# Forgetting attention: who parts queries and keys of head pairs 2 to 7 into a high and a low half

## The reference

```python
def fox_mixer(xn, w_q, w_o, k, v, c):
    q = (xn @ w_q).reshape(B, T, B_HEADS, HEAD_DIM)        # T = 512, 16 heads of 64
    for i in range(T // BLK):                              # 4 blocks of 128 queries
        q0, q1 = i * BLK, (i + 1) * BLK
        s = einsum('bqhd,bkhd->bhqk', q[:, q0:q1], k[:, :q1]) * scale
        s = s + (c_t[:, :, q0:q1, None] - c_t[:, :, None, :q1])
        s = where(causal, s, NEG)
        p = softmax(s, axis=-1)
        outs.append(einsum('bhqk,bkhd->bqhd', p, v[:, :q1]))
    return concatenate(outs, axis=1).reshape(B, T, B_WIDTH) @ w_o
```

## Time and profile before

| | |
|---|---|
| median of 3 runs | 3076.61 us (3074.89 to 3082.62) |
| profiled execution, span from its first to its last instruction | 3080.3 us |
| PE busy | 2933.2 us, 95% of the span |
| DVE busy | 1776.7 us, 58% |
| ACT busy | 1435.4 us, 47% |
| POOL (GpSimd) busy | 538.9 us, 17% |
| the 32 units of `fox` | about 2535 to 2655 us of the span |

### The profile page before, as it was taken

How to read it: one execution, slowest core, us unless ns; L and a number is a source line. 1 busy time by engine, 2 the same in 40 slices (tenths; PEclk the granted TensorE clock), 3 DMA queues, 4 the chain that set the end, 5 groups by cost and what they waited for, 6 DMA issues and landing times. The chain is left out here.

```text
span 3080.3 us, 38613 instructions
## 1 busy us (share of the span) xinstructions
PE 2933.2 (95%) x15514; PEld 2375.0 (77%) x15514; DVE 1776.7 (58%) x1996; ACT 1435.4 (47%) x1913; POOL 538.9 (17%) x626
## 2 busy tenths in 40 slices
PE   8999999898999999999999899999999998899998
PEld 4878888786887578777777478788888896688887
DVE  4448755546644788888888264555544326455543
ACT  3345525437223478888787133533333325443332
POOL 0016513224101633323222100000001002000000
PEclk9999999999999999999999999999999998899999
DMA  5220111021762599999999551233332310233331
GB/s 206 55 64 1 45 46 56 28 56 59 229 196 87 205 336 371 362 370 373 372 380 355 219 197 47 55 97 96 103 103 69 113 39 32 76 89 96 96 101 44
DMA packets 278385, 456.07 MB, mean 148 GB/s; under 512 B 24864, under 2 KB 206752, under 8 KB 258112
## 3 DMA queue, kind: packets, MB, share of 16 engines
q1 hardware_dynamic: 251712, 398.82, 37.5%
q0 software_dynamic: 26496, 54.79, 4.9%
HBM read 451.16 MB, written 39.08 MB: 159 GB/s over the span
## 5 line engine op out<-in xcount | busy, mean ns | idle before, releaser
L264 DVE TENSOR_TENSOR weight_part<-weights,weight_part 128x2048 fp32r<-128x2048 f32 (+1 forms) x62 | 140.6, 2267 | 157.0 <-ACT weight_part L253 157.0
L1193 ACT ACTIVATE up_conv<-banks,tap_columns 128x512 f32<-128x512 f32 x88 | 68.5, 778 | 292.4 <-PE banks L311 292.4
L253 ACT ACTIVATE weight_part<-weights 128x2048 fp32r<-128x2048 f32 (+1 forms) x62 | 116.0, 1871 | 172.7 <-PE banks L306 167.2
L781 POOL TENSOR_SCALAR branch_mean<-branch_mean 128x1 f32<-128x1 f32 x20 | 10.4, 521 | 1059.0 <-ACT up_conv L775 713.3
L1237 DVE SCALAR_TENSOR_TENSOR up_conv<-banks,tap_columns,up_conv 128x511 f32<-128x511 f32 x88 | 65.9, 749 | 218.0 <-ACT up_conv L1193 218.0
L306 PE MATMUL banks<-hT_r,weight_part 128*128 128x512 f32 x448 | 176.5, 394 | 0.3 <-PEq L3857 0.3
L311 PE MATMUL banks<-hT_r,weight_part 128*128 128x512 f32 x448 | 175.6, 392 | 0.0
L264 DVE TENSOR_TENSOR weight_part_o<-weights,weight_part_o 128x2048 fp32r<-128x2048 f32 (+2 forms) x46 | 100.0, 2175 | 117.8 <-ACT weight_part_o L253 117.8
L3310 POOL DMA_INDIRECT gathered<-h_tokens,block_rows x64 | 115.6, 1806 | 203.6 <-PE banks L3427 189.1
L306 PE MATMUL banks<-hT_r,weight_part_o 128*128 128x512 f32 x384 | 151.0, 393 | 0.0
L311 PE MATMUL banks<-hT_r,weight_part_o 128*128 128x512 f32 x384 | 150.2, 391 | 0.0
(11 more groups left out here) (728 smaller groups left out, 8888.6 us busy)
## 6 DMA issues: line engine op xcount, KB each, us to landing
weights<-in_w_e_gate SPq DMA_DIRECT2D x44, 1024.0 KB, 15.6
weights<-in_w_e_up SPq DMA_DIRECT2D x44, 1024.0 KB, 18.2
hT<-in_w_e_down SPq DMA_DIRECT2D x44, 1024.0 KB, 18.6
weights<-in_w_up SPq DMA_DIRECT2D x88, 512.0 KB, 5.2
gate_up<-in_w_e_gate SPq DMA_DIRECT2D x22, 1024.0 KB, 15.6
gate_up<-in_w_e_up SPq DMA_DIRECT2D x22, 1024.0 KB, 18.3
down<-in_w_e_down SPq DMA_DIRECT2D x22, 1024.0 KB, 18.3
weights<-in_w_down SPq DMA_DIRECT2D x20, 1024.0 KB, 5.0
```

What stands on the lines that cost most here:

```text
L253: c.nc.scalar.activation(self.pair(n)[0][:, 0:z], self.raw[n % RAW_SLOTS][:, 0:z], ACT.Copy).then_inc(self.high_ready, 1)
L264: c.nc.vector.tensor_tensor(low[:, 0:z], self.raw[n % RAW_SLOTS][:, 0:z], high[:, 0:z].bitcast(F32), ALU.subtract).then_inc(self.low_ready, 1)
L1193: nc.scalar.activation(a[:, f % 2, v], c.ps[:, 2 * (f % 4) + v], ACT.Identity, scale=conv[:, 2, ch:ch + 1], bias=bias[:, ch:ch + 1]).then_ ...
```

## The change

GpSimd keeps `prepare(0)` and `prepare(1)`. For pairs 2 to 7 its loop is gone. The high parts are made by ScalarE (`FoxRoom.high`): the keys' behind the exponentials of unit `4 (f - 1) + 1`, the queries' behind those of unit `4 (f - 1) + 2`. The low parts are made by VectorE (`FoxRoom.low`), at the end of its work of unit `4 (f - 1) + 2` for the keys and of unit `4 (f - 1) + 3` for the queries. TensorE waits for both low parts (`parted`) ahead of the first scores of pair `f`.

```diff
+    def high(self, c, act, f, x):
+
+        part, whole = ((self.kp, self.kT), (self.qp, self.qT))[x]
+        c.nc.scalar.activation(part[f % 2][:, 0], whole[:, f], ACT.Copy).then_inc(self.rounded, 1)
+
+    def low(self, c, dve, f, x):
+
+        part, whole = ((self.kp, self.kT), (self.qp, self.qT))[x]
+        dve.wait_ge(self.rounded, 2 * (f - 2) + x + 1)
+        c.nc.vector.tensor_tensor(part[f % 2][:, 1], whole[:, f], part[f % 2][:, 0].bitcast(F32), ALU.subtract).then_inc(self.parted, 1)
...
         def _(pool):
             room.prepare(c, pool, 1)
-            for f in range(2, KD):
-                pool.wait_ge(scored, NT * (f - 1))
-                room.prepare(c, pool, f)
...
-                    if i == 0:
+                    if i == 0 and f < 2:
                         pe.wait_ge(room.prepared, 4 * (f + 1))
+                    elif i == 0:
+                        pe.wait_ge(room.parted, 2 * (f - 1))
...
+                if n < U and n % NT in (1, 2) and 2 <= n // NT + 1 < KD:
+                    if n % NT == 1:
+                        act.wait_ge(scored, n - 1)
+                    room.high(c, act, n // NT + 1, n % NT - 1)
...
                     nc.vector.tensor_tensor(oT[1][:, f], c.ps[:, 6 + f % 2], oT[0][:, f].bitcast(F32), ALU.subtract).then_inc(left, 1)
+                if n < U and n % NT in (2, 3) and 2 <= n // NT + 1 < KD:
+                    room.low(c, dve, n // NT + 1, n % NT - 2)
```

More of the change, by code:

```diff
@@ L1382, in __init__ @@
         self.prepared = c.sem("fox_prepared")
+        self.rounded, self.parted = c.sem("fox_rounded"), c.sem("fox_parted")
     def more(self, c):
```

## The result

| | before | changed |
|---|---|---|
| median | 3078.84 us (4 runs, 3074.89 to 3082.62) | 3100.92 us (4 runs, 3098.75 to 3107.11) |
| ratio, 95% interval | | 1.0071 (1.0055 to 1.0086) |
| span of the profiled execution | 3080.3 us | 3105.4 us |
| start of the stage (pair 0's last 128x1024 maximum) | 2541.07 | 2551.83 |
| the stage, to pair 7's maximum | 98.75 us | 113.60 us |

The change makes the kernel 22 us slower. The direction and the stall are as predicted. The size was not: I had 14.0 us, and the median lies 2.9 us above the range; the term that failed is the slow clock's, and some 3 us lie outside the stage. Two profiles decompose their own difference exactly: 10.8 us in the start of the stage, 14.85 in the stage, -0.5 behind it.

What follows compares the result with a forecast made beforehand. GpSimd's subtractions delay VectorE's divisions, stalling PE and lowering its clock. Stage 11.17 + 6 x (11.17 + 3.91 stall + 1.85 clock) = 112.8 against 98.75 us; 3076.6 + 14.0 = 3090.6 us, range 3083 to 3098.

Steps and rivals of the forecast that it cites:

- What bound the kernel before: At six pair boundaries GpSimd's subtractions delay VectorE's divisions; PE stalls 1.58 us each; removing all would gain 20.6 us.
- What is hidden: ScalarE's roundings fit its idle gaps and the keys' subtraction fits VectorE's 1.44 us idle time; they cost nothing.
- The stall: Ahead of the first scores of pairs 2 to 7, PE waits 3.91 us for VectorE's queries' subtraction.
- that place: Queries' subtraction directly behind the division, ahead of the low output part: stall of 1.97 us.
- The clock: Behind each of six stalls PE's slow clock costs 1.85 us, the mean cost in the kernel before.
- My bound of 2.90: Upper bound in this stage for the slow clock's cost behind each stall, giving 20.3 us more in sum.
- The sum again: Stage from 98.75 to 112.8 us: one clean boundary and six with stall and slow clock, 14.0 us more.
- No difference: Rival: the stall comes but the slow clock costs under 1.05 us a boundary; 3079.5 to 3085.8 us, chance 0.18.
- Faster: Rival: the queries' low part is there before PE asks; 3056 us with all of it hidden, chance 0.03.
- No effect on the divisions: Rival: VectorE's long divisions have another cause than GpSimd and stay; 3098 us, chance 0.01.
- The rule set against it: Skill's advice of VectorE for elementwise work, GpSimd about twice as slow; by it alone a 20.6 us gain.

Runs made afterwards that it cites:

- pool_two_units_later: Kernel before, with GpSimd's wait for pairs 2 to 7 moved two units later; 3066.06 us, ratio 0.9949.
- pool_casts_only: Kernel before, keeping GpSimd's casts but leaving out its subtractions for pairs 2 to 7; 3063.22 us, ratio 0.9938.
- no_parting: Changed kernel without the parting of pairs 2 to 7 and PE's wait for it (leaves out work); 3065.69 us, ratio 0.9946.
- one_unit_earlier: Changed kernel with all roundings and subtractions of the parting one unit earlier; 3066.1 us, ratio 0.9947.
- the full-clock stages: For the changed kernel, the 100.23 us stage of it with 17 idle multiplications of the identity ahead of PE's wait for the parts; 3088.88 us, ratio 1.0024.
- changed_again: Changed kernel, unedited, timed and profiled again; 3103.61 us, ratio 1.0077, stage 121.83 us.
- double_subtraction_2: Changed kernel with the queries' subtraction done twice; 3118.98 us, ratio 1.0110.
- before_output_part: Changed kernel with the queries' subtraction ahead of the low output part and its wait for ScalarE; 3096.53 us, ratio 1.0040.
- samples 1 and 2: Kernel before, unedited, two further profiled executions; single-run times 3091.39 and 3083.76 us.
- the fourth profile of the changed kernel: Changed kernel, unedited, profiled once more; single-run time 3104.71 us, stage 113.65 us.

## What was right in the prediction, and the term that failed

**What bound the kernel before.** Right. GpSimd's subtractions held up the divisions; moving them (pool_two_units_later) or leaving them out (pool_casts_only) took 16 to 19 us off, against the 20.6 that I gave for the stage (its stage shrinks by 17 to 19 us from the mean of four profiles).

**What is hidden.** Right: no wait, no growth for the roundings and the keys' subtraction; no_parting and one_unit_earlier have the same stage.

**The stall.** Predicted 3.91 us each; the timeline has 3.84, and 3.71 at full clock net of idle time. Set against before's 1.45 (I had 1.58), the six make 6 x (3.71 - 1.45) = 13.6 us where the sum's stall terms came to 14.0. The layout by hand was good to 0.1 us, and it named the deciding chain: with the low output part and its wait for ScalarE out of the way the stall is 1.8 us, near the 1.97 that I gave for that place.

**The clock: the step that failed.** I took "the mean cost of now, 1.85 us", for the stalls before and after alike, so that the term fell out of the difference. With the full-clock stages as zero, it measures in the changed kernel (113.60 - 100.23) / 6 = 2.2 to (121.83 - 100.23) / 6 = 3.6 us, in the mean of four profiles (115.73 - 100.23) / 6 = 2.6; in the kernel before, whose full-clock stage would be 77.98 + 6 x 1.45 = 86.7, from 1.0 to 2.0, in the mean of four (96.95 - 86.7) / 6 = 1.7. So behind the new stall the clock costs some 0.9 us more at each boundary, 5.2 us in all. My bound of 2.90 came from the stalls of then; the mean of 2.6 lies inside it, changed_again's 3.6 does not.

That the greater length of the stall is the reason is not shown. Reckoned in the same way, with its own stall added to the 77.98 us, double_subtraction_2 pays most, (133.73 - 77.98 - 6 x 4.44) / 6 = 4.9 us behind 4.6 us; but before_output_part pays (107.59 - 77.98 - 6 x 1.69) / 6 = 3.2 us behind only 1.8, more than three of the four profiles of the changed kernel. Its stall stands where the changed kernel's does, ahead of the scores, while that of the kernel before stands ahead of the transposes. The place, or the moment at which the stall falls, may count as much as the length; no run separates them.

**The sum again.** By the means of four profiles each the stage grows from 96.95 to 115.73 us, 18.8 in place of 14.0. The medians differ by 22.1 and 21.8 us. The remaining 3.3 us lie outside the stage, where the prediction counted nothing; by the profiles they lie ahead of it, where both kernels have the same instructions: the mean start is 2546.65 before and 2549.83 changed, in ranges of 10.7 and 3.7 us that overlap. Much of the scatter comes in at the start of the experts' stage. The kernel before:

```profile
1079.69 1.09 PE L3427 MATMUL banks<-ident,gathered 128*128 128x128 f32 x8 [1.61 <-DMA gathered<-h_tokens,block_rows]
```

and the changed one, where the same transposes wait 8.00 us for the gathered rows:

```profile
1090.11 1.97 PE L3444 MATMUL banks<-ident,gathered 128*128 128x128 f32 x8 [8.00 <-DMA gathered<-h_tokens,block_rows]
```

That wait is no mark of the change: the kernel before has 7.89 and 8.01 us there in its samples 1 and 2, and double_subtraction_2 has 1.83.

Whether the change moves the mean or four profiles are too few is open, and the record points both ways. For chance: the six edited forms of the changed kernel start at 2543.30 to 2548.03 us, in the mean at 2546.4, no later than the kernel before. Against it: the fourth profile of the changed kernel starts at 2549.36 us, at 2548 or later again, which was the rival recorded for it; and one_unit_earlier and no_parting, whose stage is 19.0 us below the mean of before, are faster by only 15.3 and 15.7 us, while pool_casts_only, which keeps GpSimd's loop, has 18.6 of its 18.95. Of the 10.3 us between 3090.6 and 3100.9, then, 5.2 are the clock, 2.2 the base (3078.84 us where three runs had given 3076.61), 3.3 what lies outside the stage, and -0.4 the stall.

**The rivals.** *No difference* needed a clock that costs under 1.05 us behind the long stall; it cost at least 2.2 in the mean of every profile. *Faster* failed at the point that it named: the order of instructions puts the subtraction behind the low output part; with the order changed by one unit it came true. *No effect on the divisions* is excluded by 418 ns each.

**The rule set against it.** The Trainium skill (GPSIMD Engine Reference, Engine selection) would have had this change gain. Its ratio of the two engines' speeds is borne out (0.68 us against 1.28), and the gain is real at the right place in the queue: 15.3 us faster there, 22 us slower here. The Trainium skill (SBUF — State Buffer, SBUF: two separate sides) also says that a VectorE instruction in a two-port mode and one of GpSimd exclude each other for the whole of an instruction, by which starts first. The divisions that take 2.77 and 2.45 us where GpSimd subtracts, in the earlier trace rows and in pool_two_units_later, agree with it; which mode the divisions run in no run shows.

## What to carry to other kernels

Before giving work to a faster engine, find out when its result is asked for and what stands ahead of it in that engine's queue: here PE waited 3.8 us for a subtraction of 0.68 us, 2.0 of them for the instruction ahead of it and that one's wait for a third engine, the rest because it came after the maximum and the divisions of its unit. One unit earlier the same instructions were free. The best kernel of this case that does all of the work is one_unit_earlier, at 3066.1 us; a single changed constant in the GpSimd version reaches the same time. A stall of TensorE has a second price, the clock behind it, which is best measured by filling the stall with idle multiplications and comparing, and which one profile doesn't tell.

## What the runs showed of the hardware that I had not expected

- The slow clock's cost is no constant and doesn't follow from the length of the stall alone: 0 to 4.5 us behind stalls of 1.8 us in one execution (3.2 in the mean), 2.2 to 3.6 behind 3.8 us (means of an execution), and 4.9 behind 4.6 us.
- Within an execution it repeats closely (17.05 to 17.16 us in six windows of the first changed profile), while another execution of the same kernel has 16.8 to 19.4.
- Work without use can pay: 17 multiplications in each of six stalls made the changed kernel 15 us faster.
- The same instructions ahead of the stage ended anywhere from 2541 to 2552 us.
